# Decode attention: 32x32 block transposes on VectorE, scores as eight 64-row by 32-column tiles, four cache slots

## The reference

```
s = (q_lat . ckv + q_pe . kpe) * MLA_SCALE      # 32 x 4096, plus the 4 new tokens under a causal mask
p = softmax(s);  o = p . ckv                    # 32 x 128, then through w_uv
```

## Time and profile before

| | us |
|---|---|
| median of three runs | 2593.29 |
| the three runs | 2582.71, 2593.29, 2594.2 |
| span of the profiled execution, first to last instruction | 2590.8 |
| the profiled execution's own time beside its span | not listed |
| stage 4 of layer 0, from its first cache transpose (521.4) to its last copy (650.3) | 129 |
| stage 4 of layer 1 (1811.5 to 1940.8) | 129 |

### The profile page before, as it was taken

The page is one execution under the profiler, slowest core; times in us unless marked ns, Lnnn a source line. Parts: engine busy times, 40 slices in busy tenths (PEclk is TensorE's granted clock), DMA queues, the critical chain, the costliest instruction groups (busy, mean ns, idle before and its releaser), DMA issues.

```text
span 2590.8 us, 38420 instructions
## 1 busy us (share of the span) xinstructions
PE 2405.8 (93%) x16036; PEld 1427.4 (55%) x16036; DVE 1144.1 (44%) x2122; ACT 690.5 (27%) x1452; POOL 469.6 (18%) x566
## 2 busy tenths in 40 slices
PE   8999998899999999999899999888999999999985
PEld 5645555666666765333366455566666676733332
DVE  3355556843231345333254555567431423633334
ACT  1033444432111331111130344544321122311113
POOL 6004323410100001111260042243100000011112
PEclk9999999999999999999999999999999999999996
DMA  5001001152223228999830010011521421599996
GB/s 188 11 19 30 11 12 38 42 196 94 97 96 134 82 103 314 396 423 423 323 138 11 19 30 11 11 38 45 205 87 61 150 81 65 207 351 407 423 418 234
DMA packets 79509, 390.12 MB, mean 151 GB/s; under 512 B 20686, under 2 KB 24396, under 8 KB 59820
## 3 DMA queue, kind: packets, MB, share of 16 engines
q1 hardware_dynamic: 61180, 308.85, 31.1%
q0 software_dynamic: 17568, 76.57, 7.7%
q10 hardware_dynamic: 576, 2.10, 0.2%
HBM read 355.31 MB, written 41.41 MB: 153 GB/s over the span
## 4 chain that ended last, share of the span: by engine, by line
PE 73%; DVE 12%; ACT 4%; issue 4%; DMA 3%; PEld 2%; POOL 1%; POOLq 0%; PEldq 0%; SPq 0%; DVEq 0%; ACTq 0%
PE ps L1502 12%; PE ps L788 8%; PE ps L811 8%; PE ps L1526 6%; PE ps L1410 4%; PE ps L879 4%; PE ps L959 4%; PE ps L971 3%; DVE arena L2247 2%; PE ps L987 2%; PEld ps L811 2%; PE ps L1164 2%; PE ps L937 2%; PE ps L1488 2%; DMA arena<-yrow 1%
## 5 line engine op out<-in xcount | busy, mean ns | idle before, releaser
L1502 PE MATMUL ps<-arena 128*32 128x512 f32 x2304 | 321.2, 613 | 25.4 <-issue 19.6
L811 PE MATMUL ps<-arena,ring 128*128 128x352 f32 x936 | 281.9, 464 | 1.0 <-ACTq L483 1.0
L788 PE MATMUL ps<-x,ring 128*128 128x352 f32 x768 | 230.8, 462 | 10.9 <-DMA x<-in_x 9.4
L811 PEld LDWEIGHTS ps<-arena,ring 128*128 128x128 f32 x936 | 179.8, 192 | 101.2 <-issue 3.2
L2691 DVE COPY arena<-ps 128x1024 f32<-128x1024 f32 x44 | 53.9, 1225 | 334.6 <-PE ps L1488 334.6
L1502 PEld LDWEIGHTS ps<-arena 128*32 128x32 f32 x2304 | 93.1, 113 | 193.5 <-issue 193.5
L788 PEld LDWEIGHTS ps<-x,ring 128*128 128x128 f32 x768 | 146.5, 191 | 92.6 <-issue 12.5
L1526 PE MATMUL ps<-arena 128*32 128x512 f32 x1408 | 160.2, 595 | 3.9 <-ACT arena L1922 3.9
L2891 POOL DMA_INDIRECT arena<-xrow,arena x46 | 46.8, 1018 | 592.4 <-DVE arena L2666 319.4
L959 PE MATMUL ps<-arena 96*128 96x512 f32 (+3 forms) x384 | 147.1, 493 | 0.0
L1688 ACT ACTIVATE ring<-ps 128x512 f32<-128x512 f32 (+2 forms) x192 | 87.4, 490 | 127.0 <-PE ps L971 126.9
(11 more groups left out here) (473 smaller groups left out, 3852.2 us busy)
## 6 DMA issues: line engine op xcount, KB each, us to landing
arena<-in_w_gu SPq DMA_DIRECT2D x52, 2048.0 KB, 14.0
arena<-in_w_dn SPq DMA_DIRECT2D x64, 1024.0 KB, 11.0
ring<-in_ring SPq DMA_DIRECT2D x56, 512.0 KB, 3.7
ring<-in_w_gu SPq DMA_DIRECT2D x12, 2048.0 KB, 13.4
arena<-yrow SPq DMA_DIRECT2D x16, 1024.0 KB, 9.0
arena<-in_mem_k SPq DMA_DIRECT2D x16, 512.0 KB, 6.8
arena<-in_mem_v SPq DMA_DIRECT2D x16, 512.0 KB, 8.8
xrow<-arena SPq DMA_DIRECT2D x16, 512.0 KB, 8.2
```

What stands on the lines that cost most here:

```text
L788: mm = pe.matmul(ps[:, PIECE_BANKS[n % len(PIECE_BANKS)], 0:CH], ring[:, j % RING, k, :], x[:, k, tok], start=k == 0, stop=k == KT - 1)
L811: mm = pe.matmul(ps[:, (j % 2) * NCH + c, 0:CH], ring[:, j // per, (j % per) * units + k, :], src[:, k, tok], start=k == k0, stop=k == uni ...
L1502: mm = pe.matmul(ps[r, 2 + n % 2, :], xb_t[:, n % 2, k, r], w_gu[e % NW][:, k, :], start=k == 0, stop=k == KT - 1, skip_group_check=True)
```

## The change

- VectorE turns the cache itself: `dve.transpose` over 128x1024 turns each 32x32 block in place of its partition group, from SBUF to SBUF. Five such steps make a sequence (`STEPS`): the rotary keys (b = 0) and the four quarters of the latent dimension (b = 1 to 4). They go through a ring of three tiles (`NCT`). The PE transposes of the cache, `ring_turns`, `turn_half`, `k4` and the copies go.
- After such a transpose, each group of 32 partitions holds a 32-wide slice of the dimension for its own tokens. The scores therefore use queries that are block-diagonal over pairs of partition groups: `q8[b]`, 128 x (8 x 2 x 32). A step is two column halves x, and for each of them four column groups g and two row halves h, 64 rows by 32 columns by 256 columns each, h to a bank of its own.
- `q8[0]` (rotary) is made by VectorE in stage 2 with four copies per head; `q8[1]` to `q8[4]` are zeroed by POOL and filled by DMAs from `q_dec` on SP, four per tile (`spread_q`): 1 and 2 in stage 3, 3 and 4 in stage 4, after `g_zero` has its second increment, which comes behind `cache_load(1)` on POOL. TensorE waits for them at steps 1 and 3 of sequence 0.
- Four latent cache slots and two for the rotary keys: load n >= 2 waits until the first transpose of n - 2, load n >= 4 for the values of n - 4.
- `new_maxima` stands on VectorE at the end of iteration 0. Both copies of turned probabilities and `keep_o` are ScalarE's. In iteration n TensorE does steps 0 to 2 of n, the probabilities of n - 1, steps 3 and 4 of n, the values of n - 1.
- Several small tiles move to other places, some of them into `rope`; the tail uses bank 6 in place of 2.

```diff
-NSLOT = 3
+NSLOT = 4
+STEPS = P // KROW + 1
+NCT = 3
...
+        q8 = [view(at, DB, 2, ND) for at in (SC + 2560, SC + 1536, SC + 2048, SC + 4096, SC + 4608)]
...
+        ck = [view(at, BLK, P) for at in (XN, XN + 5120, XN + 9216, XN + 13312)]
+        kr_c = [view(at, BLK, ROPE) for at in (XN + 4096, XN + 20480)]
+        ct = view(XN + 17408, NCT, BLK, KROW)
...
+                def spread_q(b):
+
+                    for a in range(4):
+                        sp.dma_start(q8[b][KROW * a:KROW * (a + 1), :, a % 2, :], q_dec[KROW * (b - 1):KROW * b]).then_inc(kr_or_q_moved, 16)
+
                 sp.wait_ge(g_zero, 1)
+                for b in (1, 2):
+                    spread_q(b)
...
+                sp.wait_ge(g_zero, 2)
+                for b in (3, 4):
+                    spread_q(b)
                 sp.wait_ge(stage_done, 4 * (BARRIERS.index(4) + 1))
...
+                def scores(n, b):
+
+                    m = STEPS * n + b
+                    pe.wait_ge(ct_ready, m + 1)
+                    if n == 0 and b >= 1:
+                        pe.wait_ge(kr_or_q_moved, 48 + 16 * (8 if b <= 2 else 16))
+                    if b == 0 and n >= 2:
+                        pe.wait_ge(pd_ready, n)
+                    for x in range(2):
+                        for g in range(4):
+                            for h in range(2):
+                                r = slice(64 * h, 64 * (h + 1))
+                                mm = pe.matmul(ps[ND * g:ND * (g + 1), 4 + 2 * (n % 2) + h, 256 * x:256 * (x + 1)], q8[b][r, n, x, :],
+                                               ct[r, m % NCT, 8 * g:8 * (g + 1), :], start=b + x == 0, stop=b == STEPS - 1, skip_group_check=True)
+                    mm.then_inc(sc_done if b == STEPS - 1 else ct_used, 1)
+
+                def turn_probs(n):
+
+                    pe.wait_ge(pd_ready, n + 2 if n >= 1 else 1)
+                    for f in range(2):
+                        if n >= 1:
+                            pe.wait_ge(probs_taken, 2 * n - 1 + f)
+                        for j in range(4):
+                            mm = pe.transpose(ps[:, 2 + f, j * P:(j + 1) * P], pd[:, 4 * f + j, :], ident)
+                        mm.then_inc(probs_turned, 1)
...
                 for n in range(DB):
+                    for b in range(3):
+                        scores(n, b)
                     if n >= 1:
+                        turn_probs(n - 1)
+                    for b in range(3, STEPS):
+                        scores(n, b)
+                    if n >= 1:
+                        values(n - 1)
+                    else:
                         new_scores()
...
+                turn_probs(DB - 1)
+                pe.wait_ge(o_kept, DB - 1)
                 project(0, 1)
+                values(DB - 1)
...
                 for n in range(DB):
+                    probs(n)
+                    if n == 0:
+                        act.wait_ge(tail_dve, 3)
+                        act.activation(p_new, p_new, ACT.Exp, scale=MLA_SCALE).then_inc(pd_ready, 1)
+                    take_probs(n)
+                    if n >= 1:
+                        keep_o(n - 1)
...
+                def turn_keys(n, b):
+
+                    m = STEPS * n + b
+                    if b == 0:
+                        dve.wait_ge(ck_full[n % NSLOT], 32 * (n // NSLOT + 1))
+                    if m >= NCT:
+                        used, last = divmod(m - NCT, STEPS)
+                        dve.wait_ge(*((sc_done, used + 1) if last == STEPS - 1 else (ct_used, (STEPS - 1) * used + last + 1)))
+                    keys = ck[n % NSLOT][:, :, KROW * (b - 1):KROW * b] if b >= 1 else kr_c[n % 2]
+                    dve.transpose(ct[:, m % NCT], keys).then_inc(ct_ready, 1)
...
                 for n in range(DB):
+                    for b in range(STEPS):
+                        if b == 3 and n >= 1:
+                            maxima(n - 1)
+                        turn_keys(n, b)
+                    if n == 0:
                         new_maxima()
...
                 step(pool.memset(d_state, 0.0))
+                step.mark(pool.memset(q8[1], 0.0))
+                step(pool.memset(q8[2], 0.0))
                 pool.memset(g_k, 0.0).then_inc(g_zero, 1)
...
+                    if n >= 2:
+                        pool.wait_ge(ct_ready, STEPS * (n - 2) + 1)
                     if n >= NSLOT:
                         pool.wait_ge(pv_done, n - NSLOT + 1)
                     cache_load(n)
+                    if n == 1:
+                        step.mark(pool.memset(q8[3], 0.0))
+                        step.sync()
+                        pool.memset(q8[4], 0.0).then_inc(g_zero, 1)
```

More of the change, by code:

```diff
@@ L1189, in project @@
                         pe.matmul(ps[:, j * NCH + c, 0:CH], ring[:, j, k, :], mix[:, k, chunks[c][1]], start=k == PART_K, stop=k == KT - 1)
-                def latent_scores(n, h, first):
-                    bank = 4 + 2 * (n % 2) + h
-                    for j in range(4):
-                        mm = pe.matmul(ps[ND * j:ND * (j + 1), bank, :].rearrange("p (g k) -> p g k", g=4), q_dec[:, n, :],
-                                       ct[:, h].rearrange("p (g j) k -> p g j k", j=4)[:, :, j, :],
-                                       start=first, stop=not first, skip_group_check=True)
-                    return mm
@@ L1200, in rope_scores @@
-                def rope_scores(n, h, first):
-                    return pe.matmul(ps[:, 4 + 2 * (n % 2) + h, :], qpe_dec[:, n, :, :].rearrange("p j q -> p (j q)"), k4[:, h, :],
-                                     start=first, stop=not first, skip_group_check=True)
-                def half_ready(n, h, u):
-                    pe.wait_ge(turn_free[0], (u + 4) // 2)
-                    pe.wait_ge(turn_free[1], (u + 4) // 2)
-                    pe.wait_ge(k4_evac, 2 * n + h + 1)
-                def values(n, u):
-                    pe.wait_ge(turn_free[0], (u + 2) // 2)
-                    pe.wait_ge(turn_free[1], (u + 2) // 2)
+                def scores(n, b):
[12 more added lines that the diff above has]
+                    mm.then_inc(sc_done if b == STEPS - 1 else ct_used, 1)
@@ L1215, in values @@
+                def turn_probs(n):
[6 more added lines that the diff above has]
+                        mm.then_inc(probs_turned, 1)
+                def values(n):
                     if n >= 1:
@@ L1276, in _ @@
                     out = ps[:, 4 + n % 4, (n // 4) * ND:(n // 4 + 1) * ND]
-                    pe.matmul(out, o_part[:, n, :], w_sel[:, n, :], start=True, stop=False)
+                    pe.matmul(out, o_part[n], w_sel[:, n, :], start=True, stop=False)
                     mm = pe.matmul(out, ckv_tok[r, :], pn_t[r, n // 4, :], start=False, stop=True)
@@ L1827, in _, with take_probs, keep_o @@
-                probs(DB - 1)
-                take_turn(u, pdt[:, 0, :])
+                def take_probs(n):
+                    for f in range(2):
+                        act.wait_ge(probs_turned, 2 * n + f + 1)
+                        act.activation(pdt[:, f, :], ps[:, 2 + f, :], ACT.Copy).then_inc(probs_taken, 1)
+                def keep_o(n):
+                    act.wait_ge(pv_done, n + 1)
+                    act.activation(o_part[n], ps[:, value_bank(n), 0:P], ACT.Copy).then_inc(o_kept, 1)
@@ L2173, in q_pe @@
                     for j in range(4):
-                        step.mark(dve.tensor_copy(qpe_dec[32 * j:32 * j + 32, :, j, DT * h:DT * (h + 1)], src))
-                    step.mark(dve.tensor_copy(qpe_new[64:96, :, DT * h:DT * (h + 1)], src))
+                        step.mark(dve.tensor_copy(q8[0][32 * j:32 * j + 32, :, j % 2, DT * h:DT * (h + 1)], src))
                 def inverse(i, hf):
@@ L2407, in _ @@
+                    if n == 0:
+                        new_maxima()
                 dve.wait_ge(pd_ready, 1)
-                step.mark(dve.tensor_reduce(l_new[0:ND, :], p_new[0:ND], AX, ALU.add))
+                step.mark(dve.tensor_reduce(l_new[0:ND, :], p_new, AX, ALU.add))
                 maxima(DB - 1)
@@ L2809, in _ @@
                 pool.wait_ge(vg_done, NT + 1)
-                step(pool.memset(qpe_dec[:, :, :, :], 0.0))
+                step(pool.memset(q8[0], 0.0))
                 def rope_q(h, hf, cols):
@@ L2853, in cache_load @@
                 def cache_load(n):
-                    for dst, cache in ((ck[n % NSLOT], "cache_ckv"), (kr_c[n % NSLOT], "cache_kpe")):
+                    for dst, cache in ((ck[n % NSLOT], "cache_ckv"), (kr_c[n % 2], "cache_kpe")):
                         pool.indirect_dma_start(dst.rearrange("p j c -> p (j c)"), None,
```

190 lines of the change are left out of this document (52 added, 138 removed).

## The result

The changed kernel takes 2564.94 us (median of five runs, 2561.83 to 2571.45) against 2593.29 beside it: a ratio of 0.9904, 95% interval 0.9876 to 0.9931. That is 28 us less by the medians, 25 by the ratio, where 53 were forecast. The profiled execution has a span of 2563.1 us, 27.7 less than before. Counted as before, from its first cache transpose to its last copy, stage 4 of layer 0 lasts from 515.5 to 636.0 us, of layer 1 from 1798.8 to 1917.3: 120.5 and 118.6 us, against 128.9 and 129.3. So 19.1 us come from the stage, where 55 were forecast for its parts.

A forecast was written before the change was run, and what follows sets the result against it. Bound: the decode attention's chain of waits, over half of the loop being transposes and their copies. Per layer +8.1 - 32.9 - 2.7 + 1.05 = -26.5 us, two layers -53, giving 2540 us; range 2515 to 2582.

The forecast's parts named there:

- start: Stage 4 up to the values of sequence 0: waiting for the query DMAs makes them end 8.1 us later, at 557.6.
- six passes: Decode attention loop, values of sequence 0 to those of 6: 13.22 us per sequence becomes 7.73, gaining 32.9 us per layer.
- tail: From the values of sequence 6 to the stage's end: 18.75 us instead of 21.45, so -2.7 per layer.
- sum of stage 4: Stage 4 of one layer: start +8.1, loop -32.9 and tail -2.7 us together.
- rival 4: Loop: VectorE's block transpose takes twice the copy, 2.45 us, making the kernel slower at 2624 us; chance 0.08.
- rival 1: Loop scores: eight tiles don't overlap fully, TensorE paces the loop, 2561 us (2587 if row halves run serially); chance 0.22.
- Small-run DMAs land in 4.7 us: 537: Stage 4 start: the query DMAs, all issued by 532.5, land 4.7 us later, at 537, when TensorE resumes.
- rival 2: Stage 4 start: query DMAs come late, held by cache loads until some 549, +12 us a layer, 2564 us; chance 0.13.
- T = 7.7 us, six passes gain 32.9: Loop: VectorE sets 7.7 us per sequence, TensorE needing 7.4, against 13.22 before; six passes gain 32.9 us per layer.
- The fifth small query copy per head: The added copy of the query per head runs beside TensorE-bound work and costs nothing.
- Stage 3, forecast 1.05 dearer: Opening of stage 3: POOL zeroes two more tiles and TensorE's first levels wait for it, +1.05 us per layer.

The follow-up runs named there:

- e10_hold1: Changed kernel with query DMAs earlier in 1 KB runs, new tokens' maximum later, ScalarE's table loaded early, cache load 1 held until query DMAs land: 2534.9 us, ratio 0.9805.
- e3_noload: Changed kernel with cache loads 4 to 7 left out, sequences 4 to 7 computed from the data of 0 to 3: 2549.3 us, ratio 0.9849.

## Why the prediction was partly right

Values of sequence 0, values of sequence 6 and the end of the stage separate its terms. Layer 0 of the two profiled executions:

| | forecast | measured |
|---|---|---|
| start | +8.1 | 43.9 against 28.1: +15.8 |
| six passes | -32.9 | 55.2 against 79.3: -24.1 |
| tail | -2.7 | 21.3 against 21.5: -0.1 |
| sum of stage 4 | -27.5 | -8.4 |

**What was right.** The block transpose costs 1.22 us, the 1.225 of the nearest row; rival 4 is dead. Eight tiles overlap almost in full: 96 records of score tiles take 2.75 us from the start at 559.33 to the next group at 562.08, 0.46 per half step of 16 records and 0.92 per step, against 0.86 taken. The Trainium skill, "TensorE: Matmul & The Clock Gate", section "Part 3: Packing small matmuls — row/col tiling", has two thirds of the ideal for 16 tiles; for eight tiles of 64 rows this trace shows no loss of that size, so rival 1 is dead too. A pass without a load takes 7.55 us for 7.7, but there was luck in it: VectorE, forecast at 7.7, is busy 7.13 of it, and TensorE, forecast at 7.4, needs 7.55 and sets it. And the gain lies in the loop, paid for in part at the start.

**The step that failed first: "Small-run DMAs land in 4.7 us: 537".** From the end of POOL's second memset I gave the query DMAs 8.2 us (3.7 to issue, 4.7 to land); they took 15.2, from 522.5 to 537.7. Both prices came from stretches where nothing else moved; rows 7 showed that here the engines would be full. With no load in flight e10_hold1 takes 6.8 us from the first issue to the steps; beside two loads each query row took its turn with a row of theirs. That was rival 2, with a chance of 0.13. Its place was right, and so was its mechanism, a small packet that waits for a large one each time. Its price, +12 from three loads, was 5 us too high: two loads were in front, +7. The remaining 0.7 us or so of +15.8 are small: half clock for longer than taken, and 1.28 us of a table load that stood ahead of the first exponential.

**The step that failed second: "T = 7.7 us, six passes gain 32.9".** The pass exists where no load is in the way; over the six passes it takes 9.2 us on average, 8.8 us lost. I checked that TensorE's work (7.4) fits beside VectorE's (7.7), and that the cache lands in time. I did not ask how fast TensorE uses up its instructions, so their arrival was priced at nothing. Before, a pass had 137 matmul records in 13.2 us, 10 per us; now it has 232 in 7.55, 31 per us. 128 records then last 4.2 us in place of 12.3, and with the loads beside it the next ones come 1.2 to 2.3 us late. TensorE has no slack to absorb it (busy for all of 7.55), and one stop was followed by values at half clock (3.57 us for 1.95, in windows with a mean of 0.77). No rival had this. That the stops hang on the loads is shown by e3_noload. That what comes late is a block of instructions is shown by the packets of the instruction queue, which end 1.3 to 1.6 us before TensorE goes on. The density fits with the kernel before having no stop under the same loads: it uses up a block in 12.3 us, more than the 7 that the latest one takes to come.

**The tail.** I took the last values to stand under the maximum and the exponential. They do, but the projection and the 12 filler matmuls that stood there before now come behind them, and the first small transposes of the tail start 4.5 us after the last scores in place of 2.7. That is the missing 1.8; the rest is a wait of 0.91 for ScalarE's copies, as forecast, and a clock at 0.50 for the last 8 us of the stage, where it was so for some 6 before:

```profile
619.82 1.45 PE L1177 MATMUL ps<-arena,ring 128*128 128x352 f32 x4 [0.91 <-ACT arena L1795]
```

```profile
628.00:633.00 5.00, 5.00 (x17) 4.30 (x17) 0.49 (x2) 0.00 (x0) 0.00 (x0) 0.50 0.00 0
633.00:637.00 4.00, 3.51 (x21) 1.91 (x21) 0.00 (x0) 0.28 (x1) 0.00 (x0) 0.50 0.00 0
```

**Priced at nothing.** The fifth small query copy per head may not have been free: in stage 2 TensorE waits three times for another copy of VectorE, and for less long now. The same wait of the kernel before and of the changed one (225 to 420 us; us in total, times, longest):

```profile
PE ps L971 <- DVE arena L2159: 4.8, 3, 1.6
```

```profile
PE ps L985 <- DVE arena L2136: 3.6, 3, 1.2
```

That is 1.2 us a layer, in the kernel's favour; that the small copy is the reason is not shown. Stage 3, forecast 1.05 dearer, is so: from POOL's first memset to the first cache transpose it is 0.9 us longer in layer 0, 1.7 in layer 1. The rest of the difference outside stage 4 stands ahead of stage 3 of layer 0 (6.8 us with the 1.2) and behind stage 4 of layer 1 (4.2 us). In stage 2 of layer 0 the granted clock of the profiled execution before fell to 0.83 to 0.92 in five stretches of 10 us and the changed one's did not; in layer 1 it is the other way round. I do not count these to the change.

The sum of the terms is the stage's -8.4 in layer 0; layer 1's stage is 10.7 shorter. The two failed steps, +7 and +8.8, the other 0.7 of the start and the tail's 2.6 bring layer 0 from the 27.5 us that were forecast down to 8.4.

## What to carry to other kernels

A price read from a quiet stretch does not hold where a bulk transfer is in flight: ask what is queued beside a small DMA at that moment, count its rows on each DMA engine, at one row of the load each, and keep bulk loads that nobody needs yet behind it, or cut them in pieces with shorter rows. When work moves from a few wide instructions to many small ones, count the instructions per microsecond as a resource of its own beside the engine's time, above all where DMA traffic runs.

## What was not expected of the hardware

- Eight SBUF-to-SBUF DMAs of 32 KB: 5.3 us to issue in 128-byte runs with little else in flight, 10 us beside two cache loads; issued alone in 1 KB runs, landed 1.4 us after the last (e10_hold1); beside two loads, not until these were through, whether in 2048 runs of 128 B or 256 of 1 KB. Beside a load they move one row for each row of it (104 and 105 packets in 4 us).
- TensorE stops of 1.0 to 3.3 us, every 127 or 128 matmul records or a multiple of that, while the DMA engines carry 340 to 370 GB/s and TensorE starts 31 matmul records per us; none at 10 records per us under the same loads, none at 31 without loads. Each ends 1.3 to 1.6 us after a packet of 16,384 bytes of the instruction queue, which beside a load starts 3.1 to 4.9 us after TensorE began the block before, and within 0.7 us without.
